# Halves of the tokens at three norms, and projections moved behind the head of the gated stage

## The reference

```python
mix = concatenate([y_conf, y_att, y_sc, y_pool]) @ w_out      # mixer 1
h = h + rms_norm(mix, g_mix_post)
hn = rms_norm(h, g_mlp_pre)                                    # seam 1
ff = square(relu(hn @ w_up)) @ w_down
h = h + rms_norm(ff, g_mlp_post)                               # seam 2
gate = sigmoid(rms_norm(h, g_ple_pre) @ w_ple_gate)
e = (p @ w_ple_proj) * gate
h = h + rms_norm(e, g_ple_post)                                # seam 3
# the second block starts: z = rmsnorm(h, ln_mix) @ w_in_2, then attention, gated
# linear attention, two branches, w_out_2, and a convolved feed-forward of width 2816
```

## Time and profile before

| what | value |
|---|---|
| median of 3 runs | 1486.15 us (1486.03 to 1486.26) |
| profiled execution | 1487.08 us, span 1485.3 us |
| PE busy | 1461.8 us, 98% of the span |
| DVE busy | 824.8 us, 56% |
| ACT busy | 557.5 us, 38% |
| POOL busy | 223.8 us, 15% |
| mean granted TensorE clock | 0.990 |
| DMA | 129.18 MB, mean 87 GB/s |

### The profile page before, as it was taken

One profiled execution on the slowest core, in us unless ns is written; L12 is line 12 of the kernel. 1 busy time (PEld: TensorE's weight loads), 2 busy tenths in 40 slices (PEclk: granted clock), 3 DMA queues, 4 the chain that ended last, 5 costly groups with the idle time before them and its releaser, 6 DMA issues.

```text
span 1485.3 us, 17639 instructions
## 1 busy us (share of the span) xinstructions
PE 1461.8 (98%) x6978; PEld 1191.3 (80%) x6978; DVE 824.8 (56%) x1181; ACT 557.5 (38%) x829; POOL 223.8 (15%) x143
## 2 busy tenths in 40 slices
PE   9999999999999999999999999999999999999998
PEld 6766778888888887777788888888888788888887
DVE  5587467643434346765767733634442665534554
ACT  5334534522324224533455536322242443323310
POOL 4155244000000012431034201300011000000000
PEclk9999999999999999988999999999999999999999
DMA  6221123333323322312211211323332233332331
GB/s 228 86 70 59 43 86 100 99 100 95 95 95 99 99 91 69 97 57 71 72 44 53 62 43 57 100 87 98 100 100 85 63 112 109 100 100 89 106 102 58
DMA packets 36131, 129.18 MB, mean 87 GB/s; under 512 B 4024, under 2 KB 4280, under 8 KB 36048
## 3 DMA queue, kind: packets, MB, share of 16 engines
q1 hardware_dynamic: 35760, 127.78, 27.9%
q10 hardware_dynamic: 288, 0.26, 0.1%
HBM read 125.91 MB, written 2.10 MB: 86 GB/s over the span
## 4 chain that ended last, share of the span: by engine, by line
PE 87%; DVE 7%; ACT 3%; issue 2%; DMA 0%; POOL 0%; SPq 0%; DVEq 0%; ACTq 0%; POOLq 0%
PE P L1154 23%; PE P L1156 22%; PE P L1155 22%; PE P L1181 3%; PE P L1173 3%; PE P L1175 3%; DVE P L2004 1%; PE P L1439 1%; DVE WL L1845 1%; DVE WST L2225 1%; PE P L1220 1%; PE P L1276 1%; PE P L1401 1%; PE P L1482 0%; PE P L1422 0%
## 5 line engine op out<-in xcount | busy, mean ns | idle before, releaser
L1845 DVE TENSOR_TENSOR WL<-WR,WH 128x1024 fp32r<-128x1024 f32 x216 | 282.6, 1309 | 166.0 <-ACT WH L1519 165.4
L1519 ACT ACTIVATE WH<-WR 128x1024 fp32r<-128x1024 f32 x232 | 244.1, 1053 | 330.6 <-PE P L1156 266.1
L1154 PE MATMUL P<-AH,WH 128*128 128x512 f32 x872 | 352.5, 404 | 1.7 <-issue 1.7
L1156 PE MATMUL P<-AH,WL 128*128 128x512 f32 x872 | 342.2, 392 | 0.0
L1155 PE MATMUL P<-AL,WH 128*128 128x512 f32 x872 | 342.1, 392 | 0.0
L1154 PEld LDWEIGHTS P<-AH,WH 128*128 128x128 f32 x872 | 165.1, 189 | 42.5 <-issue 10.0
L1156 PEld LDWEIGHTS P<-AH,WL 128*128 128x128 f32 x872 | 165.2, 189 | 35.4
L1155 PEld LDWEIGHTS P<-AL,WH 128*128 128x128 f32 x872 | 165.4, 190 | 33.1 <-issue 0.7
L1154 PE MATMUL P<-FH,WH 128*128 128x512 f32 x432 | 168.0, 389 | 0.0
L1155 PE MATMUL P<-FL,WH 128*128 128x512 f32 x432 | 168.0, 389 | 0.0
L1156 PE MATMUL P<-FH,WL 128*128 128x512 f32 x432 | 168.0, 389 | 0.0
(11 more groups left out here) (331 smaller groups left out, 2077.5 us busy)
## 6 DMA issues: line engine op xcount, KB each, us to landing
WR<-in_ws SPq DMA_DIRECT2D x232, 512.0 KB, 3.6
out<-Y SPq DMA_DIRECT2D x8, 256.0 KB, 2.0
H<-in_xT SPq DMA_DIRECT2D x3, 512.0 KB, 8.4
C<-in_const SPq DMA_DIRECT2D x1, 946.5 KB, 11.2
H<-in_xT SPq DMA_DIRECT2D x2, 256.0 KB, 4.4
PR<-in_pT SPq DMA_DIRECT2D x1, 512.0 KB, 5.0
WR<-in_ws SPq DMA_DIRECT2D x1, 384.0 KB, 4.4
WR<-in_ws ACTq DMA_DIRECT2D x1, 128.0 KB, 3.8
```

The source lines that it names most:

```text
L1154: e.matmul(P, wh, xh, start=start, stop=False)
L1156: ins = e.matmul(P, wl, xh, start=False, stop=stop)
L1519: e.activation(m.WH[:, c % NW, :], m.WR[:, c % NRAW, :], ACT.Copy).then_inc(*at.up("w_hi", "w_hi", c))
L1845: e.tensor_tensor(m.WL[:, c % NW, :], m.WR[:, c % NRAW, :], m.WH[:, c % NW, :].bitcast(F32), ALU.subtract).then_inc(*at.up("w_lo", "w_lo", c))
```

## The change

Three stages end, and the next ones begin, by halves of 256 tokens.

- `by_halves`: the last tiles of a stage (all eight of the last part of mixer 1, which have two blocks each; tiles 6 and 7 of the down projection and of the gate) are first computed for tokens 0 to 255, each in a ring bank of its own, and then all for tokens 256 to 511, with the same converted weights. The sums, the root, the spread of the first half and its residuals for blocks 0 and 1 stand inside the second pass.
- `head_halves`: blocks 0, 1 and 2 of the head (WINDOW = 3) are taken for the first half, then for the second, and blocks 3 to 7 whole. The sums of the second half stand inside block 1 of the first half, their spread behind block 2 of it.
- The squares of the pre-norm and further residuals move behind. In seam 1 the last two squares go straight into the sums instead of one, and VectorE's addition of square 6 goes.
- All `warm` matmuls behind the first three of the kernel are gone.
- The eight projection tiles leave seam 2 and follow the gated stage's own head. The first six are read by VectorE's multiplication straight from PSUM; tiles 6 and 7 are still copied to SBUF.
- All steps of `residual`, `x_hi`, `x_lo`, `square`, `sums`, `spread`, `rsqrt`, `mix1`, `down1`, `ple_gate`, `ple_gated` take a half (`a` = 0 or 1) or the whole (`None`), and events carry the half.

```diff
+WINDOW = 3
+def cols(a):
+    return slice(0, T) if a is None else slice(T // 2 * a, T // 2 * a + T // 2)
+def parts(a):
+    return (0, 1) if a is None else (a,)
...
+    def by_halves(self, work, take, between):
+        ids, tiles = [], []
+        for k, (specs, xs) in enumerate(work):
+            ids.append([])
+            t = self.ring()
+            for j, (spec, x) in enumerate(zip(specs, xs)):
+                i = len(self.plan)
+                if j == k == 0:
+                    self.ahead(i)
+                self.plan.append(spec)
+                ids[k].append(i)
+                self.say("mm_half", t, i, x, 0, j == 0, j == len(specs) - 1)
+                self.tick()
+                if k * len(specs) + j == 4:
+                    self.rest()
+            take(k, t, 0)
+        for k, (specs, xs) in enumerate(work):
+            t = self.ring()
+            tiles.append(t)
+            for j, x in enumerate(xs):
+                i = ids[k][j]
+                if i % CH == 0 and i != ids[0][0]:
+                    self.ahead(i)
+                self.say("mm_half", t, i, x, 1, j == 0, j == len(xs) - 1)
+                self.tick()
+                for step in between.get((k, j), ()):
+                    step(tiles)
...
-        if fill is None:
-            self.say("warm", self.bank(6), 3)
...
+        def sums(a):
+            self.sums(n, direct, a)
+        def spread(a):
+            spread_to[a] = self.bank(5 - a)
+            self.say("spread", n, spread_to[a], a)
+        def make(m, a=None):
+            self.say("residual", n, m, spread_to[0 if a == 0 else 1], a)
+            self.say("x_hi", s, m, a)
...
+    def head_halves(self, s, post, specs, mid):
...
+        order = [(j, a) for a in range(2) for j in range(WINDOW)] + [(j, None) for j in range(WINDOW, 8)]
...
+        make(2, 0)
+        rest(0, 0)
+        rest(1, 0)
+        self.rest()
+        for k, (j, a) in enumerate(order):
+            for q, (t, spec) in enumerate(zip(got, specs)):
...
+                self.say("mm_hi", t, ids[j][q], (x, j), j == 0 and a == 0, a)
+                if k == 1 and q == 3:
+                    sums(1)
+                    rest(2, 0)
+            if k == 2:
+                low(*order[1], say={2: lambda: spread(1)})
+                second(0)
+                second(1)
+                rest(0, 1)
+            elif k:
+                low(*order[k - 1])
+            if k == 3:
+                second(2)
+                rest(1, 1)
+                square(0)
+            if k == 4:
+                make(3)
+                rest(2, 1)
+                square(1)
+            if 5 <= k <= 9:
+                if k < 9:
+                    make(k - 1)
+                rest(k - 2)
+                square(k - 3)
...
-        part([0, 1], 2)
-        return self.post("p1", 1)
+        self.by_halves(work, take, {
+            (0, 1): [taken(0)], (1, 0): [lambda t: sums(0)], (2, 1): [taken(1)], (3, 1): [taken(2)],
+            (4, 0): [taken(3)], (4, 1): [lambda t: spread(0), lambda t: make(0, 0)],
+            (5, 1): [taken(4), lambda t: make(1, 0)], (6, 1): [taken(5)], (7, 1): [taken(6, 7)]})
...
-        proj(range(4))
-        ready = self.post("p2", 1, [lambda: proj(range(4, 6)), lambda: proj(range(6, 8))])
+        def last_two(n, work, take):
+            sums, spread, make = post = self.post(n, 1)
+            self.by_halves(work, lambda k, t, a: take(6 + k, t, a), {
+                (0, 4): [lambda t: sums(0)],
+                (1, 3): [lambda t: spread(0), lambda t: make(0, 0), lambda t: take(6, t[0], 1), lambda t: make(1, 0)],
+                (1, 7): [lambda t: take(7, t[1], 1)]})
+            return post
...
+        gate(0, out[0])
+        for m in range(6):
+            t = proj(m)
+            if m < 5:
+                gate(m + 1, out[m + 1])
+            self.say("ple_gated", m, t)
+            self.close(t)
             self.say("square", "p3", m, 1)
...
+    def mm_half(t, i, x, a, start, stop):
+        c, wh, wl, ends = weights(i)
+        P, s = m.bank[t.bank][:, cols(a)], cols(a)
...
+        e.matmul(P, wh, xh[:, s], start=start, stop=False)
+        e.matmul(P, wh, xl[:, s], start=False, stop=False)
+        ins = e.matmul(P, wl, xh[:, s], start=False, stop=stop)
```

More of the change, by code:

```diff
@@ new lines, in head_halves, with low, rest, square @@
+    def head_halves(self, s, post, specs, mid):
+        sums, spread, make = post
+        x = "A" + s
+        got = [self.ring() for _ in specs[2:]] + [self.bank(6), self.bank(7)]
+        ids = {}
+        order = [(j, a) for a in range(2) for j in range(WINDOW)] + [(j, None) for j in range(WINDOW, 8)]
+        def low(j, a, say={}):
+            for q, (t, i) in enumerate(zip(got, ids[j])):
+                if a != 0:
+                    self.ahead(i)
+                self.say("mm_lo", t, i, (x, j), j == 7, a)
+                if q in say:
+                    say[q]()
+        def rest(m, a=None):
+            self.say("x_lo", s, m, a)
+        def square(m):
+            self.say("square", s, m, 0)
+        def second(m):
+            make(m, 1)
+        make(2, 0)
[4 more added lines that the diff above has]
+            for q, (t, spec) in enumerate(zip(got, specs)):
+                if a != 1:
+                    ids.setdefault(j, []).append(len(self.plan))
+                    self.plan.append(spec[j])
+                self.say("mm_hi", t, ids[j][q], (x, j), j == 0 and a == 0, a)
[22 more added lines that the diff above has]
+                square(k - 3)
+            if k == 9:
+                square(7)
+        low(7, None)
+        last = self.bank(5)
+        for j in range(8):
+            if j == SUMS:
+                self.sums(s, 0)
+            if j == SUMS + 4:
+                b = self.bank(4)
+                self.say("spread", s, b)
+            mid(last, j)
+        self.say("rbc", s, b)
+        return got + [last]
@@ L483, in mixer1, with take, taken @@
         self.onpool = False
-        part([0, 1], 2)
-        return self.post("p1", 1)
+        sums, spread, make = post = self.post("p1", 2)
+        def take(m, t, a):
+            self.say("mix1", m, t, 2, a)
+            self.close(t)
+            self.say("square", "p1", m, 2, a)
+        def taken(*ms):
+            return lambda t: [take(m, t[m], 1) for m in ms]
+        work = [([block("w_out", 128 * q, 128 * m) for q in (0, 1)], [("B1", 0), ("B1", 1)]) for m in range(8)]
+        self.by_halves(work, take, {
[3 more added lines that the diff above has]
+        return post
     def forget(self):
@@ L561, in up @@
             self.close(t)
-        out = self.head("2", ready, [fu(f) for f in range(6)], self.wide(fu(6), "A2"))
+        out = self.head_halves("2", post, [fu(f) for f in range(6)], self.wide(fu(6), "A2"))
         self.say("ple_in")
@@ L565, in mlp1, with down @@
         up(7, self.tile(fu(7), A))
[L567 to L570, removed]
+        def down(g, ms):
+            for m in ms:
+                t = self.tile(*fd(g, m))
                 self.say("down1", m, t, g)
@@ L577, in mlp1 @@
                 up(f, self.tile(fu(f), A))
[L578 to L585, removed]
-        proj(range(4))
-        ready = self.post("p2", 1, [lambda: proj(range(4, 6)), lambda: proj(range(6, 8))])
+            down(g - 1, range(8))
+        down(3, range(6))
@@ L604, in mlp1, with proj, gate @@
-        self.paced(*(lambda m=m: both(m) for m in range(6)))
-        for m in (6, 7):
[L606 to L612, removed]
+        out = self.head_halves("3", post, [fg(m) for m in range(5)], self.wide(fg(5), "A3"))
+        def proj(m):
+            return self.tile([block("w_ple_proj", 128 * j, 128 * m) for j in range(2)], [("P1", j) for j in range(2)])
+        def gate(m, t, a=None):
+            self.say("ple_gate", m, t, a)
+            self.close(t)
@@ L1253, in warm_first, with sums @@
         at.also(("full", t.id), "warmed")
-    def warm(t, n):
-        free(t)
-        for i in range(n):
-            ins = e.matmul(m.bank[t.bank][:], m.C[:, 0:128], m.C[:, 0:T], start=True, stop=True)
-        ins.then_inc(*at.up("full", "full", t.id))
-        at.also(("full", t.id), "read", t.id)
-    def sums(n, t, direct):
+    def sums(n, t, direct, a):
         AC = m.sq(n)[1]
```

358 lines of the change are left out of this document (202 added, 156 removed).

## The result

| | median, us | runs | profiled span, us | clock |
|---|---|---|---|---|
| before, same chip | 1486.09 (1479.49 to 1487.04) | 6 | 1485.3 | 0.990 |
| after | 1495.49 (1491.02 to 1496.85) | 6 | 1493.9 | 0.990 |

The ratio of after to before is 1.0078 (95% interval 1.006 to 1.0097): the change costs 0.6 to 1.0%, 9 to 14 us, where I had forecast 5.8 us gained. The range, 1471 to 1485.5, does not hold it.

What follows compares the result with a forecast made beforehand. TensorE, busy 98% of a 1485.3 us span, was taken as the bound. Seams of 30.85 us, less 11.6 us certain costs and the stalls, netted 5.8 us: 1480.3 us at the median, range 1471 to 1485.5.

Steps and rivals of the forecast that it cites:

- Certain costs: Extra TensorE work at the three seams: halved matmul pairs, sums and spreads; 4.47, 3.50 and 3.62, together 11.6 us.
- (a): Second half's root to its first block, in all seams: an uncovered wait of 1.55 us, 1.7 in seam 2.
- (d): First sums wait 0.4 in seam 1, 0.25 in seam 3; block 3 waits 1.2 in seam 2, about 0.1 elsewhere.
- (c): First half's spread to blocks 0 and 1: stalls 0.95, 0.5, 0.5; block 1 adds 0.55 (seam 2), 0.95 and 0.45 (seam 3).
- (b): Second sums to second spread: VectorE's root starts late behind its queue, stalling 0.05, 1.4 and 1.05 us by seam.
- Rival C: TensorE's clock falls once, with seam warm matmuls removed and short waits between halves: 3.4 us lost, 1483.7; chance 0.09.
- A: The forecast itself, all seams: 5.8 us gained, 1480.3 us, own range 1476 to 1483; chance 0.50.
- seam 2 waits 1.45 and keeps 1.00: Argument against a clock fall: in the kernel before, seam 2 has a 1.45 us bare wait yet keeps full clock.
- Its filler is gone: Seam 2, down projection to gated stage, loses 4.89 us because the projection tiles that lay inside it move out.
- Rival E: Seam 3's first sums still wait for GpSimd's running sum, 3.76 us before; 4 of 8.2 us lost, 1484.3; chance 0.08.
- Rival D: VectorE and GpSimd block each other where the second root is due, 2.44 us per seam: 1487.6, slower; chance 0.07.
- B: VectorE's queue is shorter than assumed, only 6.3 us of stalls remain: 13.0 us gained, 1473.2; chance 0.26.

Runs made afterwards that it cites:

- e1: Changed kernel with block 3's residual and high part issued ahead of the weight chunk's conversion in each halved head; 1491.90 us, 1.0050 of before.
- e3: Changed kernel with block 3 issued early and the pending weight low parts moved behind the first sums; 1486.53 us, 1.0017 of before.
- e12: e5 without any warm matmuls at the three seams; 1491.58 us, 1.0053 of before.
- e5: Kernel before, whole at all seams, with only the eight projection tiles moved behind the gated stage's head; 1483.06 us, 0.9988 of before.
- e16: Kernel before with 7 warm matmuls instead of 3 ahead of seam 3's sums; 1482.55 us, 0.9992 of before.
- e6: e3 with seam 2 whole again, six projection tiles inside it and two behind the head; 1482.38 us, 0.9987 of before.
- e8: e6 with all eight projection tiles inside seam 2, none behind the head; 1482.85 us, 1.0001 of before.
- e17: e10 with 5 warm matmuls instead of 3 ahead of seam 3's sums; 1478.66 us, 0.9967 of before.
- e10: Kernel before, no halves, with six projection tiles inside seam 2 and two behind the gated stage's head; 1481.39 us, 0.9987 of before.
- e15: Kernel before with 24 warm matmuls instead of 3 ahead of seam 3's sums; 1495.30 us, 1.0086 of before.
- e4: Changed kernel with three warm matmuls inside block 1 of each halved head, where it waits for its weight; 1493.84 us, 1.0068 of before.
- e13: Kernel before, four projection tiles behind the gated head, 12 warm matmuls ahead of seam 3's sums, 6 ahead of seam 2's; 1491.38 us, 1.0054.
- e14: e10 with 16 warm matmuls instead of 3 ahead of seam 3's sums; 1491.55 us, 1.0046 of before.

## Why the prediction was wrong

- **Certain costs (11.6 us): right.** Pairs run at 0.12 in after as in the earlier trace rows, and seam 1 closes with them: 9.98 - 4.47 - 8.5 of waits is -3.0, near the 2.7 us by which the point is later. By the formula of the Trainium skill ("TensorE: Matmul & The Clock Gate", section Back-to-back issue gap) 256 columns are estimated at 109 ns; the rows of both kernels show 0.12 us at full clock.
- **(a), the second half's root to its first block: right.** 1.46, 1.58 and 1.46 us (219.06 to 220.88, less 0.36, in seam 1) against 1.55, 1.7 and 1.55.
- **(d), the step that failed most.** The prediction put block 3's wait at "with six tiles about 0.1 each". It was 2.80 and 2.81 us in seams 1 and 3. I added up the durations on each queue but not what a queue waits for: the converted buffers, of which two passes hold all four. In seam 2, where I had 1.2 for block 3, it waits nothing, and 1.18 came at block 5. e1 and e3 show how much hangs on it: with block 3 served first the next blocks stand behind the same chunk, and in seam 1 1.9 of the 2.80 us move on to them.
- **(c): right within 0.4.** First blocks of the first half: 1.12, 0.73 and 1.53 us against 0.95, 1.05 and 1.90.
- **(b): wrong in place and size.** No spread waits for a root in after. There are two low parts in front of the head's blocks, not one (642.97, 2.35 us for two, in seam 3), and block 1 waits for them: 1.39, 1.13 and 2.09 us, against 0.05, 1.4 and 1.05, so 4.6 in sum against 2.5.
- **Rival C was true twice.** I gave the removal of the warm matmuls no price in A, and C 0.09. The rows at 0.54 and 0.50 above are its sign: halves that start 0.21 apart instead of 0.12, some 1.5 us in seam 2 and 3 in seam 3. The sentence "seam 2 waits 1.45 and keeps 1.00" was a poor guard: here the clock fell behind 0.89 and 1.94 us of bare wait. (The wait in front of the low clock in the earlier trace rows is 3.76 us, not 3.3.) With whole seams the warm matmuls are worth more, 8.5 us (e12).
- **By seam, waits and lost pace:** some 8.5, 7.9 and 11.9 us, forecast 3.05, 5.35 and 5.05. The misses add up to some 15 us, and between forecast and result lie 15.2.
- **What I booked for the halves belongs elsewhere.** "Its filler is gone" was right for seam 2, and bigger: 6.7 us. But I cost the projections' move near nothing at seam 3, and it is worth 7.2 there by itself (e5): about 3.8 is the wait for GpSimd's sum, which it hides, and 3.0 the clock (e16). So the halves had only the rest of the seam to shorten, and as changed did not. The rows said so: 3.76 of the 16.91 waited for POOL, at a clock of 0.50, and neither needs halves to mend.
- **Rival E did not happen:** no first sums of seam 3 wait in after, since the projections stand between. It does happen where two or none do (e6, e8), with the 2.77 and 4.55 us above.
- **Rival D did not happen** as put: the second root waits nowhere and the low parts at the heads run at 1.18 each. **B** was refuted by the waits.
- TensorE did not wait between projection tiles: the three tiles' lead was enough.

Open: the halves together with warm matmuls of the right length. e3, which has none, is 0.29% above e5 and 0.36% below e12; its fixed points give 1.6 us and -3.0. A version of seams 1 and 3 whose first three blocks fit three chunks wasn't tried either.

## What to carry to other kernels

Splitting work in two passes doubles the time that its weights stay in their buffers: before adding up durations on a queue, ask for each entry what it waits for, and which entries stand behind it. Price what goes out with the change (fillers, warm matmuls) as carefully as what comes in, seam by seam, by moving one thing alone. A bare wait that cannot be removed can cost less if matmuls of just its length stand in it: seam 3 of e16 became 3.0 us shorter so, and e17 gained 5 us with two moved tiles and two more warm matmuls. Removing the cause of one wait is worth only what the next wait on the same queue leaves of it (e1).

## What the runs showed of the hardware

- TensorE fell to half its clock behind bare waits of 0.9 to 2.6 us (after, e1, e3, e10 to e12); pairs of halves then took 0.21 and whole matmuls 0.43 us each. The Trainium skill ("TensorE: Matmul & The Clock Gate", section Wait — 56ns, not 53.3ns?) has N / 1.2 GHz for a cold array, by which 512 columns take 427 ns and 256 columns, an estimate from it, 213, and these traces agree.
- A bare wait does not always bring the fall. Behind block 3's 2.65 us in the kernel after the clock was 1.00 (230 to 236 and 662 to 668). Behind 1.94 us in seam 3 it was 0.50 in after and 1.00 in e1. What decides it is open, so a low stretch seen in one profile is no fixed cost.
- A warm matmul on plain fp32 data (128x512) takes 0.86 us at full clock, and shows as two entries 0.43 apart (48 over 20.6 us in e15), against 0.2265 for one of the product's. I missed that twice, in e4 and in e13 to e15.
- The clock also falls with TensorE never idle. In 19 of the 20 profiled kernels a low stretch begins within the same eight matmuls or up to about 1 us behind them, with no idle time of TensorE in the view. Their rows say 16*128 where others say 128*128. In e5:

```profile
690.67 4.06 PE L1361 MATMUL P<-PT,GKU 16*128 16x512 f32 x8
```
```profile
700.00:710.00 10.00, 10.00 (x38) 8.44 (x37) 1.52 (x6) 7.28 (x5) 0.00 (x0) 0.62 0.19 52
```

How long it stays low differs: 0.66 over 690 to 700 in e16, and 0.57 over 695 to 715 in e14. The exception is e3, with the same eight matmuls:

```profile
690.00:715.00 25.00, 25.00 (x123) 19.42 (x122) 18.05 (x26) 12.76 (x13) 0.00 (x0) 1.00 0.20 62
```

Executions of one kernel differ by about 1.1 us per 0.001 of mean clock: before ran from 1478.22 at 0.997 to 1487.14 at 0.989. Whether they differ in this place isn't shown, since each kernel has one profile.
